# Feed-forward input product of a hybrid decoder: 18 of 22 gate/up pairs in a seven-product block form

## The reference, cut to what matters

```python
def ffn_half(h, g_pre, g_post, w_in, w_out):
    a = rmsnorm(h, g_pre) @ w_in
    gate, up = jnp.split(a, 2, axis=-1)
    return h + FFN_RESID * rmsnorm((jax.nn.silu(gate) * up) @ w_out, g_post)
```

## Time and profile before

| | us |
|---|---|
| median of 3 runs | 2437.1 |
| lowest and highest | 2434.26, 2438.48 |
| span of the profiled execution | 2438.0 |
| PE busy | 2378.5 (98%) |
| DVE, ACT, POOL busy | 828.6, 784.9, 834.6 (32 to 34%) |

### The profile page before, as it was taken

One profiled execution on the slowest core, in us unless ns is written; L12 is line 12 of the kernel. 1 busy time (PEld: TensorE's weight loads), 2 busy tenths in 40 slices (PEclk: granted clock), 3 DMA queues, 4 the chain that ended last, 5 costly groups with the idle time before them and its releaser, 6 DMA issues.

```text
span 2438.0 us, 39450 instructions
## 1 busy us (share of the span) xinstructions
PE 2378.5 (98%) x15328; PEld 2158.4 (89%) x15328; DVE 828.6 (34%) x1877; ACT 784.9 (32%) x1586; POOL 834.6 (34%) x441
## 2 busy tenths in 40 slices
PE   8999999999889999999999999999999999999998
PEld 8999988986556899998889999888999789999987
DVE  4223300586421533330053232004565644232101
ACT  5223212614322632322252322224422444222222
POOL 3333333240312333333324333331344223333332
PEclk9999999999998999999999999999999999999999
DMA  3222222232671222222222222222211432222222
GB/s 122 83 83 81 94 78 87 69 108 79 195 237 52 73 84 82 82 94 79 87 70 87 78 86 86 87 79 79 77 57 53 148 95 79 79 86 80 93 82 86
DMA packets 74906, 220.29 MB, mean 90 GB/s; under 512 B 9405, under 2 KB 26302, under 8 KB 74527
## 3 DMA queue, kind: packets, MB, share of 16 engines
q1 hardware_dynamic: 71710, 208.09, 26.8%
q0 software_dynamic: 3072, 10.49, 1.3%
HBM read 210.73 MB, written 7.82 MB: 90 GB/s over the span
## 4 chain that ended last, share of the span: by engine, by line
PE 86%; DVE 4%; SPq 3%; ACT 3%; issue 2%; DMA 2%; POOL 1%; DVEq 0%; ACTq 0%; POOLq 0%
PE psum L1758 18%; PE psum L1760 18%; PE psum L1759 18%; PE psum L1890 7%; PE psum L1892 7%; PE psum L1891 7%; PE psum L1883 2%; PE psum L1884 2%; SPq L442 1%; PE psum L2244 1%; ACT y L665 1%; SPq L493 1%; DVE y L1190 1%; SPq L458 1%; PE psum L2162 1%
## 5 line engine op out<-in xcount | busy, mean ns | idle before, releaser
L1047 POOL TENSOR_TENSOR w_lo<-raw,w_hi 128x1024 fp32r<-128x1024 f32 (+1 forms) x317 | 759.0, 2397 | 1378.4 <-ACT w_hi L651 1378.3
L1758 PE MATMUL psum<-x_hi,w_hi 128*128 128x320 f32 (+1 forms) x3312 | 986.2, 298 | 0.7 <-POOL w_lo L1047 0.5
L1760 PE MATMUL psum<-x_hi,w_lo 128*128 128x320 f32 (+1 forms) x3312 | 981.2, 296 | 0.0
L1759 PE MATMUL psum<-x_lo,w_hi 128*128 128x320 f32 (+1 forms) x3312 | 981.2, 296 | 0.0
L1758 PEld LDWEIGHTS psum<-x_hi,w_hi 128*128 128x128 f32 x3312 | 629.9, 190 | 4.0 <-POOL w_lo L1047 1.9
L1759 PEld LDWEIGHTS psum<-x_lo,w_hi 128*128 128x128 f32 x3312 | 629.9, 190 | 0.2
L1760 PEld LDWEIGHTS psum<-x_hi,w_lo 128*128 128x128 f32 x3312 | 629.7, 190 | 0.0
L651 ACT ACTIVATE w_hi<-raw 128x1024 fp32r<-128x1024 f32 (+1 forms) x323 | 339.9, 1054 | 828.5 <-DMA raw<-ffn_out 375.9
L1268 DVE TENSOR_TENSOR work<-psum,r_pre 128x256 f32<-128x256 f32 (+1 forms) x352 | 160.3, 457 | 660.4 <-PE psum L1760 658.2
L1890 PE MATMUL psum<-w_hi,gu_hi 128*128 128x512 f32 x704 | 275.0, 391 | 0.6
L1891 PE MATMUL psum<-w_hi,gu_lo 128*128 128x512 f32 x704 | 274.0, 389 | 0.0
(11 more groups left out here) (274 smaller groups left out, 2077.7 us busy)
## 6 DMA issues: line engine op xcount, KB each, us to landing
raw<-ffn_in SPq DMA_DIRECT2D x176, 512.0 KB, 3.6
raw<-ffn_out SPq DMA_DIRECT2D x88, 512.0 KB, 3.5
raw<-gla_in SPq DMA_DIRECT2D x25, 512.0 KB, 3.6
cache<-cache POOLq DMA_DIRECT2D x64, 160.0 KB, 5.2
cache<-cache SPq DMA_DIRECT2D x64, 160.0 KB, 5.4
c_k<-cache_kt SPq DMA_DIRECT2D x64, 128.0 KB, 3.4
raw<-mla_wo SPq DMA_DIRECT2D x8, 512.0 KB, 3.6
raw<-gla_wo SPq DMA_DIRECT2D x8, 512.0 KB, 3.6
```

The lines of the kernel that those rows point to most:

```text
L1047: pool.tensor_tensor(w_lo[slot][:, 0:w], raw[slot][:, 0:w], w_hi[slot][:, 0:w].bitcast(F32), ALU.subtract).then_inc(s_lo, 1)
L1758: pe.matmul(out, wh, xh, start=start, stop=False)
L1759: pe.matmul(out, wh, xl, start=False, stop=False)
L1760: return pe.matmul(out, wl, xh, start=False, stop=stop)
```

## The change

Of the 22 pairs of a feed-forward input, the first `CLASSIC` = 4 stay as they were. The other 18 (`GRP`) are made in a block form after Strassen and Winograd: the pair's weights are cut in four (gate or up, first or second half of k: a11, a12, a21, a22; each 128 x 512, 256 KB), the input in four (half of k, 288 of the 576 token columns), and seven products of 4 steps of k take the place of eight. Six are in three-matmul form; the seventh, of a22, is in plain fp32, without any split. Sums of weight parts (s1 to s4, each 128 x 512) are made by VectorE, and so are all the low parts of these groups. Sums of input parts are made once a stage, over the space of `h`, which is stored to DRAM before (`keep`) and loaded back for the output phase. In the groups GpSimd does nothing; in the first pairs and in the other stages it works as before. The up half is no longer multiplied by `r_pre`: VectorE multiplies silu(gate) with the PSUM bank directly, and the post-norm's epsilon term takes up the factor (`h_q`, two small operations a stage). Loops of instructions are written out. Several semaphores are merged (for example `s_table` into `s_mla_c`, and the eight `g_load` into four), and some buffers are moved.

The core of the diff. SyncE's loads of a group, and the places:

```diff
+HALF = TOK // 2
+GU_LO = TOK + DEC_BATCH * DEC_SEQ
 OUT_W = D_MODEL // 2
 ORDER = (0, 1, 4, 2, 3)
 SLOTS = 4
...
+                def part(dst, row_of, c, landed, g, i):
+                    sp.dma_start(dst[:, :], w_in[f, FB + 2 * g + row_of + 4 * i, :, c * HK * P:(c + 1) * HK * P]).then_inc(landed, 16)
+
+                def four(g, i):
+
+                    a = g0 + g
+                    if g >= 2:
+                        sp.wait_ge(f_p, 7 * (a - 1) + 14 * i)
+                    part(w[f"a22_{g % 2}"], 1, 1, f_a2[g % 2], g, i)
+                    sp.wait_ge(f_sum, 4 * (a - 1) + 3 + 8 * i)
+                    sp.wait_ge(f_alo, 2 * a + 4 * i)
+                    part(w["a12"], 0, 1, f_a12, g, i)
+                    sp.wait_ge(f_sum, 4 * a + 8 * i)
+                    part(w["a21"], 1, 0, f_a2[g % 2], g, i)
+                    part(w["a11"], 0, 0, f_a11, g, i)
+
+                classic_out(sp, st, 0)
+                wait_keep(sp, st)
+                part(w["a21"], 1, 0, f_a2[0], 0, 0)
+                part(w["a22_0"], 1, 1, f_a2[0], 0, 0)
+                part(w["a11"], 0, 0, f_a11, 0, 0)
+                classic_out(sp, st, 2)
+                part(w["a12"], 0, 1, f_a12, 0, 0)
+                classic_out(sp, st, 3)
+                four(1, 0)
+                for i in range((GRP - 2) // 2):
+                    four(2, i)
```

VectorE's steps of a group, with their waits:

```diff
+                def add(dst, x, y, a, used, i):
+
+                    if a > 0:
+                        dve.wait_ge(f_p, 7 * (a - 1) + used + 14 * i)
+                    dve.tensor_tensor(w[dst][:, :], w[x][:, :], w[y][:, :], ALU.add).then_inc(f_sum, 1)
+
+                def sum_1(g, i):
+                    a = g0 + g
+                    dve.wait_ge(f_a2[g % 2], 32 * (GRP // 2 * f + g // 2 + 1) + 32 * i)
+                    add("s1", "a21", f"a22_{g % 2}", a, 2, i)
...
+                    dve.wait_ge(f_sum, 4 * a + 1 + 8 * i)
+                    dve.wait_ge(f_a11, 16 * (a + 1) + 32 * i)
...
+                def low_form(name, g, hi, summed, i):
...
+                    dve.wait_ge(f_hi, 6 * a + hi + 12 * i)
+                    dve.wait_ge(f_sum, 4 * a + summed + 8 * i)
+                    dve.tensor_tensor(w[f"{name}_lo"][:, :], w[name][:, :], w[f"{name}_hi"][:, :].bitcast(F32),
+                                      ALU.subtract).then_inc(f_lo, 1)
...
+                def part_low(name, g, order, used, i):
+
+                    a = g0 + g
+                    dve.wait_ge(f_hi, 6 * a + order + 12 * i)
+                    if a > 0:
+                        dve.wait_ge(f_p, 7 * (a - 1) + used + 14 * i)
+                    dve.tensor_tensor(w[f"{name}_lo"][:, :], w[name][:, :], w[f"{name}_hi"][:, :].bitcast(F32),
+                                      ALU.subtract).then_inc(f_alo, 1)
...
+                def plus(c, ps, a, copied, product, i):
+
+                    dve.wait_ge(f_e, 3 * a + copied + 6 * i)
+                    dve.wait_ge(f_p, 7 * a + product + 14 * i)
+                    dve.tensor_tensor(c[:, :], ps[:, 0:HALF], c[:, :], ALU.add).then_inc(f_c, 1)
+
+                def scaled(c, half, evicted, i):
+
+                    dve.wait_ge(f_c, evicted + 10 * i)
+                    dve.tensor_tensor(c[:, :], c[:, :], r_pre[:, half * HALF:(half + 1) * HALF], ALU.mult).then_inc(f_c, 1)
+
...
+                def group(g, i, more):
+                    a = g0 + g
+                    if g > 0:
+                        last_half(g - 1, i)
+                    low_form("s4", g, 4, 3, i)
+                    if g > 0:
+                        low_part(g - 1, c_1[(g - 1) % 2], 2 * a, 0, i)
+                    low_form("s3", g, 6, 4, i)
+                    part_low("a12", g, 5, 6, i)
+                    if g == 0:
+                        x_low_form(1, 3)
+                    if more:
+                        sum_1(g + 1, i)
+                    plus(c_2, ring(st, g, 1), a, 3, 4, i)
+                    scaled(c_2, 1, 5 * a + 1, i)
+                    if more:
+                        sum_2(g + 1, i)
+                    dve.wait_ge(f_e, 3 * a + 2 + 6 * i)
+                    dve.wait_ge(f_p, 7 * a + 5 + 14 * i)
+                    dve.scalar_tensor_tensor(out=c_3[:, :], in0=ring(st, g, 0)[:, 0:HALF], scalar=-1.0, in1=c_3[:, :], op0=ALU.mult,
+                                             op1=ALU.subtract).then_inc(f_c, 1)
+                    dve.wait_ge(s_silu, c0 + 2 * a + 1 + 4 * i)
+                    dve.wait_ge(f_c, 5 * a + 3 + 10 * i)
+                    dve.tensor_tensor(c_2[:, :], c_2[:, :], c_3[:, :], ALU.mult).then_inc(f_gu, 1)
+                    if more:
+                        part_low("a11", g + 1, 1, 1, i)
+                        low_form("s1", g + 1, 2, 2, i)
+                        sum_4(g + 1, i)
+                    plus(c_1[g % 2], ring(st, g, 2), a, 1, 6, i)
+                    scaled(c_1[g % 2], 0, 5 * a + 4, i)
+                    if more:
+                        sum_3(g + 1, i)
+                    low_part(g, c_2, 2 * a + 1, 1, i)
+                    if more:
+                        low_form("s2", g + 1, 3, 3, i)
+
```

ScalarE's steps of a group:

```diff
+                def group(g, i, more):
+                    a = g0 + g
+                    if g > 0:
+                        last_half(g - 1, i)
+                    hi_sum("s3", a, 4, 5, i)
+                    if g > 0:
+                        high_part(g - 1, c_1[(g - 1) % 2], 2 * a, 0, i)
+                    if a >= 2:
+                        act.wait_ge(s_gulo, c0 + 2 * (a - 1) + 4 * i)
+                    if g == 0:
+                        act.wait_ge(s_gulo, c0 + 2 * a)
+                    copy_out(c_1[g % 2], ring(st, g, 0), a, 1, i)
+                    if g == 0:
+                        act.wait_ge(s_unit, u0 + 4 * CLASSIC)
+                        x_form(1, 6)
+                    if a >= 1:
+                        act.wait_ge(f_gu, 2 * a - 1 + 4 * i)
+                    copy_out(c_3, ring(st, g, 1), a, 2, i)
+                    if a >= 1:
+                        act.wait_ge(s_gulo, c0 + 2 * a - 1 + 4 * i)
+                    copy_out(c_2, ring(st, g, 0), a, 3, i)
+                    if more:
+                        hi_a11(a + 1, i)
+                        hi_sum("s1", a + 1, 1, 2, i)
+                    else:
+                        split(b0 + FB)
+                    gate(c_2, 5 * a + 2, i)
+                    if more:
+                        hi_sum("s2", a + 1, 2, 3, i)
+                    high_part(g, c_2, 2 * a + 1, 1, i)
+                    if more:
+                        hi_sum("s4", a + 1, 3, 4, i)
+                        hi_a12(a + 1, i)
+
```

TensorE's steps of a group:

```diff
+                def product(out, name, x, fresh):
+
+                    for k in range(HK):
+                        c = slice(k * P, (k + 1) * P)
+                        hi, lo = w[f"{name}_hi"][:, c], w[f"{name}_lo"][:, c]
+                        for y, m, first, end in ((hi, x[0], k == 0, False), (hi, x[1], False, False), (lo, x[0], False, k == HK - 1)):
+                            last = pe.matmul(out[:, 0:HALF], y, m[:, k, :], start=fresh and first, stop=end, skip_group_check=not fresh)
+                    last.then_inc(f_p, 1)
+
+                def group(g, i):
+                    a = g0 + g
+                    b_a, b_c, b_b = (ring(st, g, j) for j in range(3))
+                    if g < 2:
+                        pe.wait_ge(s_evicted, u0 + 4 * CLASSIC - RING + 3 * g + 3)
+                    pe.wait_ge(f_alo, 2 * a + 1 + 4 * i)
+                    if g >= 2:
+                        pe.wait_ge(f_gu, 2 * (a - 1) + 4 * i)
+                    product(b_a, "a11", b_11, True)
+                    pe.wait_ge(f_lo, 4 * a + 1 + 8 * i)
+                    if g >= 2:
+                        pe.wait_ge(f_c, 5 * (a - 2) + 1 + 10 * i)
+                    if g == 0:
+                        pe.wait_ge(f_tlo, 3 * f + 1)
+                    product(b_c, "s1", t_1, True)
+                    pe.wait_ge(f_lo, 4 * a + 2 + 8 * i)
+                    pe.wait_ge(f_e, 3 * a + 1 + 6 * i)
+                    if g == 0:
+                        pe.wait_ge(f_tlo, 3 * f + 2)
+                    product(b_a, "s2", t_2, False)
+                    pe.wait_ge(f_lo, 4 * a + 3 + 8 * i)
+                    pe.wait_ge(f_e, 3 * a + 2 + 6 * i)
+                    product(b_c, "s4", b_22, False)
+                    pe.wait_ge(f_lo, 4 * a + 4 + 8 * i)
+                    pe.wait_ge(f_e, 3 * a + 3 + 6 * i)
+                    if g == 0:
+                        pe.wait_ge(f_tlo, 3 * f + 3)
+                    product(b_a, "s3", t_3, False)
+                    pe.wait_ge(f_alo, 2 * a + 2 + 4 * i)
+                    if g >= 2:
+                        pe.wait_ge(f_c, 5 * (a - 2) + 4 + 10 * i)
+                    product(b_b, "a12", b_21, True)
+                    pe.wait_ge(f_c, 5 * a + 3 + 10 * i)
+                    pe.wait_ge(f_a2[g % 2], 32 * (GRP // 2 * f + g // 2 + 1) + 32 * i)
+                    if g == 0:
```

(87 more changed lines are left out.)

434 lines of the change are left out of this document (271 added, 163 removed).

## The result

The changed kernel takes **2521.05 us** (median; 2513.43 to 2523.63), the kernel before 2437.79 (2434.26 to 2443.21) on the same chip: a ratio of 1.033, with a 95% interval of 1.030 to 1.035. It is 3.3% slower, 83 us. The forecast was 2490 us, 52 us slower, with a range of 2420 to 2560. The profiled execution has a span of 2521.9 us at a granted clock of 0.991 (before: 2438.0 and 0.994), so the spans differ by 83.9 us.

What follows compares the result with a forecast made beforehand. TensorE, busy 98%, was taken to bound the kernel; VectorE's 10.1 us of work plus a 3.4 us load wait would make groups 13.5 us, +13.1 a stage, four times +52 on the 2437.1 median: 2490 us, range 2420 to 2560.

Steps and rivals of the forecast that it cites:

- TensorE, 11.54 us a group: Block-form groups: six products of 1.6 us and a plain fp32 seventh of 1.94, 1.26 us less than a pair.
- no wait at all: Case of the shorter-round rival (chance 0.17): 11.7 us a group, 261.8 a stage's input, -20 a stage, 2358 us.
- VectorE, 10.1 us of work: VectorE in a group: ten operations of 512 columns, 6.05 us, and nine of about 288 columns, 4.09 us.
- The wait that is added, 3.4 us: VectorE's next first sum waits for a21, issued only after VectorE's low part of a12; bounds 2.4 and 4.1 us.
- 2.95 us from the issue of a21: Time taken from SyncE's issue of a21 to its landing, within the 3.4 us wait of VectorE.
- TensorE's waits of 1 us in two places: Each group: before the third product, for s2's low part and ScalarE's bank a copy; before the seventh, for `c_3`.
- The sum: Stage's feed-forward input: 51.2 + 17 x 13.5 + 12.5 + 1.5 = 294.7 us against 281.6, +13.1, four times +52.
- a late start of 1.5: Group 0 of a stage: input sums make VectorE start some 3 us late, which costs 1.5 us once.
- The turning point, 12.7 us: Round of a group at which the change neither gains nor loses; each 0.1 us is 7 us of the kernel.
- The faster kernel: Rival: a21 there in time or VectorE's operations closer, TensorE sets the pace, round under 12.7 us; chance 0.17.
- The longer round of 14.6 us: Rival: a wait of 4.1 us and 0.02 us more an operation in the groups, 2565 us; chance 0.17.
- The clock: Rival: TensorE's gaps in the groups lower its clock to 1.2 GHz, 3105 us, or 2567 for an eighth; chance 0.03.

Runs made afterwards that it cites:

- e1: Against the changed kernel, SyncE issues the next group's a21 and a11 ahead of a12 and its wait: 2374.45 us, ratio 0.973.
- e2: Against the changed kernel, SyncE issues a11 before a21, both still behind a12, so a21 comes last: 2573.36 us, ratio 1.056.
- e5: Against the changed kernel, VectorE makes the next group's first sum behind the fourth product's addition and scaling, loads unchanged: 2498.84 us, ratio 1.025.
- e8: Against e4, GpSimd's low part of a12 also waits for VectorE's low part of s3 and next first sum: 2381.01 us, ratio 0.975.
- e6: Against the changed kernel, a21 and a11 ahead of a12, and the first sum behind the fourth product's addition and scaling: 2414.68 us, ratio 0.990.
- e7: Against the changed kernel, only a21 is issued ahead of a12; a11 stays behind it and its wait: 2422.77 us, ratio 0.992.
- e4: Against the changed kernel, a21 and a11 ahead of a12, and GpSimd instead of VectorE makes a12's low part: 2453.67 us, ratio 1.005.
- e3: Against the changed kernel, GpSimd instead of VectorE makes a12's low part in the groups, load order unchanged: 2460.25 us, ratio 1.009.

## Why the prediction was right, and where its sizes were off

**TensorE, 11.54 us a group: right.** In e1, where nothing else is late, the round is 11.77 us, and the forecast gave 11.7 for "no wait at all". Matmuls of 288 columns start 0.133 us apart (270.22, 270.36, 270.49 in the trace), and the seventh product takes 1.94 (from its first matmul to the second one of the next product 2.07 in e1, less one distance of 0.133). What e1's kernel gains, 64 us, is less than the 80 of that rival: a stage's input is 268.2 us in it, 16.3 shorter than before instead of 20. The rival's sum left out the ends of the stage.

**VectorE, 10.1 us of work: right.** The round of 13.89 us less its waits for loads of 3.85 leaves 10.04.

**The wait that is added, 3.4 us: the mechanism right, the size short.** It is the loop that was named: `f_alo`, SyncE, a21 behind a12, the first sum. e1 takes out the order and all of the wait goes; e2 lengthens the queue and the wait grows; e5 puts work ahead of it and it shrinks to 0.7. The first sum waited 251.9 us in 68 rounds, 3.70 each, and 13 times the second sum waited for a11 besides (9.9 us, 0.15 a round). The failed term is "2.95 us from the issue of a21": the round above has 3.38 from the start of that issue to the sum, and on the mean of 68 groups a21 landed 3.32 us after its issue began, 0.37 more than the term. The nearest rows were loads whose issues took 0.33 us. Here three loads are issued back to back; the issue of a21 took 0.43 us as a rule, 0.81 in the round shown and at most 1.30. That a11 is issued behind it and can be late too was not counted. The Trainium skill, "DMA: Bandwidth & Descriptors", section "Anatomy of one DMA", gives 2.0 us plus bytes over 436 GB/s, 2.6 us for such a load, but for DMAs that GpSimd issues, and these are SyncE's. a22, which is issued by itself, landed after 2.56 us on the mean, near that figure; a12, a21 and a11, issued one behind the other, took 2.93, 3.32 and 3.80. With 2.6 us for a21 the forecast would have been further off.

**TensorE's waits of 1 us in two places: right.** Before the seventh product it is 1.1 us (78.1 us in 70). Before the third it is 1.0 us for the weight load (72.3 in 69) and 0.8 for the matmul (50.6 in 65). What ends the latter is the copy of bank a, one of the two causes that the prediction named; the low part of s2 is made by then (270.95 + 0.69 us in the round shown, the matmul at 272.92).

**The sum.** 0.4 us a round more than forecast, 17 rounds: 6.8 us a stage. A stage lost 21.1 us on average where 13.1 was forecast, so 1.2 us a stage remain. In the first stage's group 0 TensorE waits about 5 us, where a late start of 1.5 was allowed: most of it 1.89 us before the third product, for the low part of s2, and 2.29 before the seventh, for `c_3`. Why VectorE was late there was not followed up. GpSimd, the `h` reload and the first output block cost nothing, as forecast: outside the input the traces agree.

**The turning point, 12.7 us, and 7 us for each 0.1 us of the round: right.** The kernels give a scale of it:

| kernel | round us | time us | ratio |
|---|---|---|---|
| e8, e1 | 11.75, 11.77 | 2381.0, 2374.5 | 0.975, 0.973 |
| e6, e7 | 12.36, 12.37 | 2414.7, 2422.8 | 0.990, 0.992 |
| e4, e3 | 12.84, 12.84 | 2453.7, 2460.3 | 1.005, 1.009 |
| e5 | 13.53 | 2498.8 | 1.025 |
| changed kernel | 13.89 | 2521.1 | 1.033 |
| e2 | 14.65 | 2573.4 | 1.056 |

From e1 to e2 it is 198.9 us for 2.88 us of round, 6.9 per 0.1. The sign turns between 12.37 and 12.84, where 12.7 was forecast.

**The rivals.** The faster kernel was a real alternative with the mechanism given for it: it is e1, one load order away. The longer round of 14.6 us is e2's, at 2573 us where 2565 was worked out. The clock played a small part that was put at nothing: in three of the 72 groups the seventh product fell to the lower level of 1.2 GHz and took 2.92 to 3.25 us to the next start, where 1.73 to 1.83 is usual. TensorE's timeline in the changed kernel, a slow group and then a usual one:

```profile
1556.40 3.87 PE L2347 MATMUL psum<-t_f,a_r 128*128 128x288 f32 x8 [2.22 <-DVE c L1628]
1559.65 0.78 PE L2307 MATMUL psum<-x_hi,a_hi_r 128*128 128x288 f32 x1
...
266.73 2.21 PE L2347 MATMUL psum<-t_f,a_r 128*128 128x288 f32 x8 [0.73 <-DVE c L1628]
```

After 2.22 us of idle time the product took 3.25 us to the next start; the usual one takes 1.83 (266.73 to 268.56). The idle time alone does not decide: one of the three fell after 1.80 us, and another group, with 2.29 us of idle time (at 86.1 us), did not. Two of the three lie in the 64 rounds counted, which took 15.04 and 15.23 us against 13.85 for the others, so some 3 us of the kernel go with the clock. A fourth fall, at 1355.4 us, lies in the third stage's group 0. The prediction had it that nothing would change unless TensorE were idle for longer than here; the clock did fall, and in e2, with longer waits, it did so in 17 rounds.

## What to carry to other kernels

Where an in-order queue loads several buffers, look at each load's wait for what the waiting engine must first do, and at what stands behind it in the queue: a load that is ready to go behind one that waits for VectorE makes VectorE pay the whole landing, every round. The busy shares (here 92% and 53%) do not show it; the list of SyncE's own waits does. Order the loads by who needs them first and by whose buffer is free first. And before work is moved to an idle GpSimd, see what VectorE does at that moment.

## What was not expected of the hardware

- A VectorE subtraction of 224 columns with both inputs in SBUF took 1476 to 1490 ns instead of 384 when it started during GpSimd's of 512 columns (1363 ns on the mean), in 68 of 68 such groups of e3; 384 ns in the four groups without overlap, and 383 in e8, where the two were kept apart.
- A third 256 KB load ahead on the same queue delayed the one waited for by 0.93 us, though an issue by itself takes 0.33 us and the DMA engines' share was only 0.23 to 0.24 in those stretches. In the changed kernel the issues of a21 and a11, right behind that of a12, took 0.43 us, that of a21 in four cases 0.81 to 1.30.
- TensorE's granted clock fell in single groups (0.88 in 13.9 us of e2) while the span's mean stayed at 0.98 or above, after idle times of 1.80, 2.04 and 2.22 us in the changed kernel, and did not fall after one of 2.29.
